# 24 of 36 expert blocks beside the top-key search in three rounded passes, split by ScalarE and GpSimd

## The chip, the cores and the metric

The kernel runs on one core of a Trainium2 chip. The metric is the device time of one launch in microseconds; the runs of one kernel are compared by their median.

## The reference, cut to what matters

Two blocks of a network follow each other over 256 tokens of width 1024. Each of the two layers of the second block ends in a product-key expert layer. Every token picks, for each of 8 heads, 16 of 16,384 experts, and only those count:

```python
cand_s = top_s[:, :, 0, :, None] + top_s[:, :, 1, None, :]      # 16 x 16 sums of the best keys of either half
best_s, best_pos = lax.top_k(cand_s.reshape(c, PEER_HEADS, -1), PEER_TOPK)
idx = jnp.take_along_axis(cand_i.reshape(c, PEER_HEADS, -1), best_pos, axis=-1)
gate = jax.nn.softmax(best_s, axis=-1)
ue = u[idx]
ve = v[idx]
act = jax.nn.gelu(jnp.einsum('td,thkd->thk', xc, ue).astype(jnp.float32), approximate=False)
return jnp.einsum('thk,thkd->td', (gate * act).astype(xc.dtype), ve)
```

## The kernel before, in words

The kernel gathers no rows. It computes the products of all tokens with all experts, densely, in 128 blocks of 128 experts, and multiplies by a matrix G that holds the gates and is zero elsewhere. A block has a u part (dot products of 256 tokens with 128 experts), a gelu, a product with its slice of G, and a v part (128 rows of 1024 added up, times the gated values).

In each layer l the expert layer goes through these stages, in this order on TensorE:

1. `wq`: the query projection, then the key scores (L2237), copied out of PSUM by ScalarE (L2345).
2. `pre`: the u parts of `EARLY` = 32 blocks, two to a chunk of weights, 16 chunks. These are plain float32 products of the weights as they landed with the float32 tokens `HX` (L2247). ScalarE applies the gelu (L2352). Meanwhile VectorE searches the best keys (function `top16`: L2421 to L2431), first over 128 keys in two turns, each framed by copies (L2442, L2445, L2446); then it adds the pairs of best keys in 16 additions (L2452), searches again over 256 sums, and works out indices and gates (L2460 to L2486). Its last step lets TensorE turn the indices around (L2254).
3. `mid`: G is built, 64 groups of four tokens, from one-hot matrices that VectorE (L2502), GpSimd (L2414) and ScalarE (L2373, L2375) write and TensorE multiplies (L2279). ScalarE copies out the part of G whose gelu does not exist yet (L2388); VectorE multiplies the part of the 32 early blocks with the gelus that `pre` left there (L2493). Between the groups TensorE does the u parts of `MID` = 8 more blocks (L2265).
4. `peer`: the `MAIN` = 88 other blocks, u part and v part in one go (L2316, L2318, L467 to L469).
5. `post`: the v parts of the 40 blocks whose u parts were done in `pre` and `mid`.

Products in `wq`, `peer` and `post` are made of three passes. ScalarE writes a rounded copy of a quarter of a chunk (a unit of 512 columns, L446), VectorE the remainder (L451), both into the buffer `SPLIT` with room for 4 units, and TensorE multiplies high by high, high by low and low by high. A chunk is 1 MB, four lie in the ring `wring`, and the SyncE queue loads the next one when `chunk_done` of its slot is raised: by TensorE in `pre` and `mid`, by VectorE behind the last remainder in the others. The semaphores `split_hi`, `split_lo` and `unit_used` count units written, remainders written and units used.

`HX_A` and `HX_B` are copies of the tokens for `mid`, written by ScalarE ahead of the early gelus (L2346, L2347). `HX_A` and the one-hot matrices lie in the same memory as `SPLIT`. GpSimd has nothing to do between the rotary tables, loaded once near a fifth of the span, and the first one-hot matrices of `mid`.

Of the kernel before, what the change touches and what calls it, by code (L numbers as in the profile page):

```python
# [16 lines left out]
ALU = mybir.AluOpType  # L17
# [8 lines left out]
T = 256  # L26
# [14 lines left out]
ROWS = 2 * PEER_HEADS  # L41
TOP = 16
BLOCKS = NKEYS
EARLY, MID = 32, 8
KEPT = MID + EARLY
MAIN = BLOCKS - KEPT
ALPHA = (2 * DEPTH) ** 0.25
# [36 lines left out]
def program(nc, A, out):  # L84
    ctx = ExitStack()
    with ctx:
# [287 lines left out]
        def turns(e, n):  # L374

            full, rest = divmod(n, RING)
            if full > 1:
                with e.Fori(0, full) as i:
                    for j in range(RING):
                        yield i, j  # L380
            else:
                for j in range(full * RING):
                    yield 0, j
            for j in range(rest):
                yield full, j
# [16 lines left out]
        def wait_done(e, name, i, j):  # L402
            s, r = slot_of(name, i, j)
            e.wait_ge(chunk_done[s], r + 2)
# [15 lines left out]
        def stream_pairs(sp, name, src, first, n):  # L420
            for i, j in turns(sp, n):
# [2 lines left out]
                sp.dma_start(wring[:, s, :].rearrange("p (a c) -> p a c", a=2),  # L424
                             src[first + RING * i + j]).then_inc(w_landed[s], 16)

        SPLIT_PHASES = [(name, n if name[:4] != "proj" else 17 - SPLIT_FROM) for name, n, _ in PHASES
                        if name != "ada" and name[:3] not in ("pre", "mid")]
        split_first, at = {}, 0
        for name, n in SPLIT_PHASES:  # L430
            split_first[name] = at
# [2 lines left out]
        def unit_of(name, i, q):  # L434

            return split_first[name] + UNITS * RING * i + q

        def raw_quarter(name, i, j, q):
            return wring[:, slot_of(name, i, j)[0], q * UNIT:(q + 1) * UNIT]
# [8 lines left out]
        def lo_quarter(v, name, i, j, q, n, buf, last):  # L448

            v.wait_ge(split_hi, n + 1)  # L450
            v.tensor_tensor(SPLIT[:, buf, 1, :], raw_quarter(name, i, j, q), SPLIT[:, buf, 0, :].bitcast(F32),  # L451
                            ALU.subtract).then_inc(split_lo, 1)
            if last:
                v.drain().then_inc(chunk_done[slot_of(name, i, j)[0]], 1)
# [67 lines left out]
        def hi_chunk(act, name):  # L522
            def work(i, j):
                for q in range(UNITS):
                    hi_quarter(act, name, i, j, q, unit_of(name, i, UNITS * j + q), q)
            return work
# [13 lines left out]
        def wait_product(e, name, i, j):  # L540

            e.wait_ge(unit_used, unit_of(name, i, UNITS * j + UNITS - 1) + 1 + UNITS)
# [1684 lines left out]
        def peer_tensor(pe, l):  # L2227
# [10 lines left out]
                                   WD["keys"], start=True, stop=True)  # L2238
                mm.then_inc(sc_done, 1)

            for i, j in turns(pe, EARLY // 2):
                w = wait_chunk(pe, f"pre{l}", i, j)
                b, u = bank_of(f"pre{l}", i, j)
                pe.wait_ge(bank_free[b], u + 1)
                for e in range(2):
                    for k in range(KT):
                        mm = pe.matmul(bank[b][:, e * T:(e + 1) * T], w[:, (e * KT + k) * P:(e * KT + k + 1) * P],  # L2247
                                       HX[:, k, :], start=(k == 0), stop=(k == KT - 1))
                mm.then_inc(chunk_done[slot_of(f"pre{l}", i, j)[0]], 1)
# [83 lines left out]
        def peer_scalar(act, l):  # L2333
            name = f"peer{l}"

            def drain_q(i, j):
                b, _ = bank_of(f"wq{l}", i, j)
                wait_product(act, f"wq{l}", i, j)
                act.activation(pairs(Q8)[:, j, :], bank[b][:, :], ACT.Copy).then_inc(bank_free[b], 1)

            ahead(act, 4, hi_chunk(act, f"wq{l}"), drain_q, started=True)
            act.drain().then_inc(q8_ready, 1)
            for f in range(8):
                act.wait_ge(sc_done, 8 * l + f + 1)
                act.activation(SC[:, 4 * f:4 * f + 4, :], view(bank[2 + f % 4][:, :], 4), ACT.Copy).then_inc(sc_in, 1)  # L2345
            act.activation(HX_A, HX[:, 0:5, :], ACT.Copy)  # L2346
            act.activation(HX_B, HX[:, 5:KT, :], ACT.Copy).then_inc(hx_kept, 1)  # L2347

            def early(i, j):
                b, _ = bank_of(f"pre{l}", i, j)  # L2350
                wait_done(act, f"pre{l}", i, j)
                act.activation(pairs(G)[:, (MAIN + MID) // 2 + RING * i + j, :], bank[b][:, :], ACT.Gelu).then_inc(bank_free[b], 1)  # L2352

            last = EARLY // 2 // RING - 1
            with act.Fori(0, last) as i:
                for j in range(RING):
                    early(i, j)
            early(last, 0)
            act.wait_ge(gate_in, l + 1)
            act.activation(IJG[:, 0, :], IJG[:, 0, :], ACT.Exp).then_inc(gate_exp, 1)  # L2360
            for j in range(1, RING):
                early(last, j)
            for tt in range(2):
                act.wait_ge(ijt_done, 2 * l + tt + 1)
                a = act.activation(PAIR[:, :, tt * P:(tt + 1) * P], view(bank[2 + tt][:, 0:3 * P], 3), ACT.Copy)  # L2365
            a.then_inc(pair_ready, 1)
            act.drain()

            def hots_scalar(n):

                act.wait_ge(g_done, GROUPS * l + n + 1)
                t = 4 * (n % 2) + 1
                act.activation(NEAR[:, n % 2, :], iota, ACT.Abs, scale=-1.0, bias=pair[:, 2, n // 2, t, :])  # L2373
                act.drain()
                act.activation(OHB[:, t, :], NEAR[:, n % 2, :], ACT.Relu, scale=-1.0, bias=ones[:, 0:1]).then_inc(hot_c, 1)  # L2375

            def mid_out(e):
                b, _ = bank_of(f"mid{l}", 0, e)
                wait_done(act, f"mid{l}", 0, e)
                act.activation(pairs(ACTX)[:, e, :], bank[b][:, :], ACT.Gelu).then_inc(bank_free[b], 1)  # L2380

            hots_scalar(0)
            hots_scalar(1)
            for n in range(GROUPS):
                if n + 2 < GROUPS:
                    hots_scalar(n + 2)
                act.wait_ge(g_done, GROUPS * l + n + 3)
                act.activation(G4[:, n, :, 0:MAIN + MID], view(bank[4 + n % 4][:, :], 4)[:, :, 0:MAIN + MID],  # L2388
                               ACT.Copy).then_inc(g_in, 1)
                if n % 16 == 1 and n > 1:  # L2390
                    mid_out(n // 16 - 1)
            mid_out(MID // 2 - 1)
            if l + 1 < DEPTH:
                act.drain()
                act.dma_start(wide_t[:], A["wide"][l + 1]).then_inc(wide_in, 16)

            def gelu(i, j):
                b, _ = bank_of(name, i, j)
                act.wait_ge(dots_ready, MAIN * l + RING * i + j + 1)
                act.activation(GA, GA, ACT.Gelu).then_inc(bank_free[b], 1)  # L2400

            peer_units(act, name, lambda *a: hi_quarter(act, name, *a),
                       begin=lambda: act.wait_ge(unit_used, unit_of(name, 0, 2) + UNITS), after=gelu)
            act.activation(TSD[:, 0:1], C["epsh"], ACT.Sqrt)
            for i, j in turns(act, KEPT // 2):
                hi_chunk(act, f"post{l}")(i, j)

        def peer_pool(pool, l):
            pool.wait_ge(pair_ready, l + 1)
# [24 lines left out]
        def peer_vector(v, l):  # L2434
# [89 lines left out]
            def gate(i, j):  # L2524
# [7 lines left out]
                v.drain()  # L2532
                v.tensor_tensor(g_lo, GA, g_hi.bitcast(F32), ALU.subtract).then_inc(gp_ready, 1)  # L2533

            peer_units(v, name, lambda i, j, q, n, buf: lo_quarter(v, name, i, j, q, n, buf, q == 3), middle=dots, late=gate)
            name = f"post{l}"

# [10 lines left out]
            def post(i, j, mid):  # L2548
                for q in range(UNITS):
                    if q % 2 == 0:  # L2550
                        kept(i, j, q // 2, mid)
                    lo_quarter(v, name, i, j, q, unit_of(name, i, UNITS * j + q), q, q == UNITS - 1)

            for j in range(MID // 2):
                post(0, j, True)
            with v.Fori(0, EARLY // 2 // RING) as i:
                for j in range(RING):
                    post(i + 1, j, False)

        block = ctx.enter_context(nc.Block())  # L2560

# [34 lines left out]
        @block.gpsimd  # L2596
        def _(pool):
            pool.wait_ge(ada_rows, ADA_EARLY)
            pool.dma_start(hyc_t[:, 0:hyc_n - T], A["hyc"][:, 0:hyc_n - T]).then_inc(hyc_in, 16)
            with pool.Fori(0, ADA_LATE) as c:  # L2600
                pool.wait_ge(late_done, c + 1)
                pool.dma_start(LATE, A["w_ada"][ADA_EARLY + c]).then_inc(late_landed, 16)
            squares_pool(pool)
            pool.wait_ge(part_lo, 3 * UNITS)
            pool.dma_start(rope_t, A["rope"]).then_inc(rope_in, 16)
            for l in range(DEPTH):
                peer_pool(pool, l)

        @block.scalar
# [260 lines left out]
```

## Time and profile before

| | |
|---|---|
| median of 3 runs | 3173.22 us (3163.9 to 3174.16) |
| the profiled run, its own time | 3169.45 us |
| its span in the trace | 3167.8 us |
| TensorE, VectorE, ScalarE, GpSimd busy | 3037.3, 2368.0, 1508.8, 216.3 us |

The profile is one execution. TensorE's busy time counts matmuls that overlap in the pipeline, so 96% busy is not 96% of its peak. All times of the trace are counted from the start of the span. A float32 matmul stands in the trace as two instructions. Layer 0's expert stages lie from 1196 to 2045 us, those of layer 1 some 1107 us later.

### The profile page before, as it was taken

What the parts mean: (1) busy time and instruction counts of PE and PEld (TensorE: products, weight loads), DVE (VectorE), ACT (ScalarE), POOL (GpSimd) and SP (SyncE); (2) the same over time, 40 slices, a digit from 0 to 9 for tenths busy, and PEclk for the clock granted to TensorE, in tenths of its full rate; (3) what the DMA queues carried; (4) which work ended last, traced back from release to release, by engine and by line L of the source; (5) the groups of instructions that cost most, each with busy time, mean ns of one, the idle gap of its engine ahead of it and who ended that gap; (6) DMA issues with size and microseconds to landing.
All of it is one profiled execution on the core that took longest, in us unless ns stands there. A gap on an engine that the chain in (4) does not pass through costs nothing.

```text
span 3167.8 us, 50781 instructions
## 1 busy us (share of the span) xinstructions
PE 3037.3 (96%) x16104; PEld 2527.0 (80%) x16104; DVE 2368.0 (75%) x5173; ACT 1508.8 (48%) x2634; POOL 216.3 (7%) x348
## 2 busy tenths in 40 slices
PE   7999999989989899999999999998999999999998
PEld 4888887869887779877888888777788778888887
DVE  5778787456657767997777777677679977777776
ACT  3222223245744652295555554446523955555544
POOL 0000000000000000190000000000001910000000
PEclk9999999999999999999999999999999999999999
DMA  7333333224222234314555555533343145555553
GB/s 271 105 114 105 114 117 109 80 73 145 80 94 105 99 130 135 131 41 159 187 188 190 189 186 188 170 107 107 120 141 125 41 146 185 186 189 189 190 188 131
DMA packets 73920, 439.61 MB, mean 139 GB/s; under 512 B 7184, under 2 KB 8720, under 8 KB 31824
## 3 DMA queue, kind: packets, MB, share of 16 engines
q1 hardware_dynamic: 71136, 419.15, 38.1%
q0 software_dynamic: 2528, 18.02, 1.6%
q8 instruction: 65, 1.06, 0.1%
q10 hardware_dynamic: 144, 0.98, 0.1%
q14 instruction: 47, 0.39, 0.0%
HBM read 437.08 MB, written 1.05 MB: 138 GB/s over the span
## 4 chain that ended last, share of the span: by engine, by line
PE 77%; DVE 15%; ACT 2%; DVEq 2%; issue 2%; ACTq 0%; DMA 0%; POOL 0%; SPq 0%
PE bank L467 16%; PE bank L469 16%; PE bank L468 16%; PE bank L2316 10%; PE bank L2318 5%; DVE arena L2502 2%; PE bank L2279 1%; DVE arena L1557 1%; PE bank L875 1%; DVE arena L2431 1%; DVE arena L2424 1%; DVE arena L2425 1%; PE bank L1505 1%; PE bank L864 1%; PE bank L1225 1%
## 5 line engine op out<-in xcount | busy, mean ns | idle before, releaser
L446 ACT ACTIVATE peer_r<-wring 128x512 fp32r<-128x512 f32 x1280 | 797.7, 631 | 797.5 <-PE bank L469 517.8
L451 DVE TENSOR_TENSOR peer_r<-wring,peer_r 128x512 fp32r<-128x512 f32 x1280 | 870.1, 692 | 408.9 <-ACT peer_r L446 405.6
L2316 PE MATMUL bank<-res_r,peer_r 128*128 128x512 f32 x1408 | 502.7, 397 | 3.4 <-DVE peer_r L451 3.4
L467 PE MATMUL bank<-h_r,peer_r 128*128 128x512 f32 (+1 forms) x1088 | 397.6, 365 | 22.6 <-DVE h_r L662 16.0
L467 PE MATMUL bank<-peer_r 128*128 128x512 f32 x1024 | 404.7, 395 | 3.2 <-DVE peer_r L2533 3.2
L469 PE MATMUL bank<-peer_r 128*128 128x512 f32 x1024 | 401.5, 392 | 0.0
L468 PE MATMUL bank<-peer_r 128*128 128x512 f32 x1024 | 399.6, 390 | 0.0
L2318 PE MATMUL bank<-res_r,peer_r 128*128 128x256 f32 x1408 | 394.9, 280 | 0.0
L469 PE MATMUL bank<-h_r,peer_r 128*128 128x512 f32 (+1 forms) x1088 | 385.4, 354 | 0.0
L468 PE MATMUL bank<-h_r,peer_r 128*128 128x512 f32 (+1 forms) x960 | 335.0, 349 | 0.0
L2316 PEld LDWEIGHTS bank<-res_r,peer_r 128*128 128x128 f32 x1408 | 264.5, 188 | 67.1 <-DVE peer_r L451 4.0
L2414 POOL TENSOR_SCALAR arena<-const_t,arena 128x128 f32<-128x128 f32 x320 | 198.6, 635 | 1679.4 <-ACT arena L2365 1666.6
L2318 PEld LDWEIGHTS bank<-res_r,peer_r 128*128 128x128 f32 x1408 | 265.6, 189 | 6.7
L467 PEld LDWEIGHTS bank<-h_r,peer_r 128*128 128x128 f32 x1088 | 207.5, 191 | 68.9 <-issue 36.9
L469 PEld LDWEIGHTS bank<-h_r,peer_r 128*128 128x128 f32 x1088 | 207.4, 191 | 28.2
L467 PEld LDWEIGHTS bank<-peer_r 128*128 128x128 f32 x1024 | 192.1, 188 | 47.0 <-DVE peer_r L2533 3.1
L469 PEld LDWEIGHTS bank<-peer_r 128*128 128x128 f32 x1024 | 192.1, 188 | 46.0
L2247 PE MATMUL bank<-arena,wring 128*128 128x256 f32 x1024 | 221.3, 379 | 0.0
L468 PEld LDWEIGHTS bank<-peer_r 128*128 128x128 f32 x1024 | 192.6, 188 | 36.0
L2247 PEld LDWEIGHTS bank<-arena,wring 128*128 128x128 f32 x1024 | 194.6, 190 | 26.5
L468 PEld LDWEIGHTS bank<-h_r,peer_r 128*128 128x128 f32 x960 | 183.3, 191 | 23.6 <-issue 2.4
L2279 PEld LDWEIGHTS bank<-arena 128*128 128x128 f32 x1024 | 127.7, 195 | 59.4 <-DVE arena L2502 52.8
(388 smaller groups left out, 4582.1 us busy)
## 6 DMA issues: line engine op xcount, KB each, us to landing
wring<-in_w_peer SPq DMA_DIRECT2D x256, 1024.0 KB, 4.9
wring<-in_w_proj SPq DMA_DIRECT2D x34, 1024.0 KB, 4.9
wring<-in_w_hy SPq DMA_DIRECT2D x32, 1024.0 KB, 5.1
arena<-in_w_ada POOLq DMA_DIRECT2D x16, 1024.0 KB, 5.2
wring<-in_w_out SPq DMA_DIRECT2D x16, 1024.0 KB, 4.9
wring<-in_w_ada SPq DMA_DIRECT2D x8, 1024.0 KB, 11.2
wring<-in_w_hyout SPq DMA_DIRECT2D x8, 1024.0 KB, 4.9
wring<-in_w_q SPq DMA_DIRECT2D x8, 1024.0 KB, 4.9
```

Of the source, the lines that this page charges most:

```text
L446: act.activation(SPLIT[:, buf, 0, :], raw_quarter(name, i, j, q), ACT.Copy).then_inc(split_hi, 1)
L451: v.tensor_tensor(SPLIT[:, buf, 1, :], raw_quarter(name, i, j, q), SPLIT[:, buf, 0, :].bitcast(F32), ALU.subtract).then_inc(split_lo, 1)
L467: pe.matmul(out_ap, w_hi, x_hi, start=start, stop=False, **kw)
L468: pe.matmul(out_ap, w_hi, x_lo, start=False, stop=False, **kw)
L469: return pe.matmul(out_ap, w_lo, x_hi, start=False, stop=stop, **kw)
L864: mm = pe.matmul(bank[b][:, f * 256:(f + 1) * 256], HC[m][:, f * P:(f + 1) * P], UT[:, part * 256:(part + 1) * 256], start=True, stop=True)
L2247: mm = pe.matmul(bank[b][:, e * T:(e + 1) * T], w[:, (e * KT + k) * P:(e * KT + k + 1) * P], HX[:, k, :], start=(k == 0), stop=(k == KT - 1))
L2279: mm = pe.matmul(bank[4 + b][:, s * P:(s + 1) * P], OHA[:, t, :], OHB[:, t, :], start=True, stop=True)
L2316: pe.matmul(two_parts(acc[:, :]), SPLIT[:, buf, 0, w], h_both[:, k, :, :], start=(k == 0), stop=False, skip_group_check=True)
L2318: mm = pe.matmul(acc[:, T:2 * T], SPLIT[:, buf, 1, w], h_hi[:, k, :], start=False, stop=(k == KT - 1), skip_group_check=True)
L2414: a = pool.tensor_scalar(OHB[:, 4 * half + s, :], iota, pair[:, 2, i, 4 * half + s, :], None, ALU.is_equal)
L2502: a = v.tensor_scalar(OHA[:, t, :], iota, pair[:, 1, 2 * i + b // 2, t, :], pair[:, 0, 2 * i + b // 2, t, :], ALU.is_equal, ALU.mult)
```

## The change

`EARLY` grows from 32 to 36, so `pre` has 18 chunks and `MAIN` shrinks from 88 to 84 blocks; `post` has 44. The first `PRE_SPLIT` = 12 chunks of `pre` (24 blocks) are done in three passes: ScalarE rounds the weights (`hi_chunk`), GpSimd writes the remainders in place of VectorE (`pre_pool`), TensorE runs `chunk3` with `h_hi` and `h_lo2`. GpSimd raises `chunk_done` for these chunks. The other 6 chunks stay as they were. ScalarE rounds the first chunk ahead of the score copies and writes `HX_A` only when the split chunks are through, because `SPLIT` is in use until then. The exponential of the gates moves to behind the gelu of chunk 14.

```diff
-EARLY, MID = 32, 8
+EARLY, MID = 36, 8
+PRE_SPLIT = 12
...
+        split_chunks = lambda name, n: {"proj": 17 - SPLIT_FROM, "pre": PRE_SPLIT}.get(name[:-1], n)
...
-            for i, j in turns(pe, EARLY // 2):
+            name = f"pre{l}"
+            for i, j in turns(pe, PRE_SPLIT):
+                chunk3(pe, name, i, j, h_hi, h_lo2, T, KT)
+            name = f"peer{l}"
+            for n in range(PRE_SPLIT, EARLY // 2):
+                i, j = divmod(n, RING)
                 w = wait_chunk(pe, f"pre{l}", i, j)
...
+            pre_hi = hi_chunk(act, f"pre{l}")
+            pre_hi(0, 0)
             for f in range(8):
                 act.wait_ge(sc_done, 8 * l + f + 1)
                 act.activation(SC[:, 4 * f:4 * f + 4, :], view(bank[2 + f % 4][:, :], 4), ACT.Copy).then_inc(sc_in, 1)
-            act.activation(HX_A, HX[:, 0:5, :], ACT.Copy)
-            act.activation(HX_B, HX[:, 5:KT, :], ACT.Copy).then_inc(hx_kept, 1)
+            act.activation(HX_B, HX[:, 5:KT, :], ACT.Copy)
...
+            ahead(act, PRE_SPLIT, pre_hi, early, started=True)
+            act.activation(HX_A, HX[:, 0:5, :], ACT.Copy).then_inc(hx_kept, 1)
+            for n in range(PRE_SPLIT, EARLY // 2):
+                early(*divmod(n, RING))
+                if n == EARLY // 2 - 4:
+                    act.wait_ge(gate_in, l + 1)
+                    act.activation(IJG[:, 0, :], IJG[:, 0, :], ACT.Exp).then_inc(gate_exp, 1)
...
+        def pre_pool(pool, l):
+            name = f"pre{l}"
+            pool.wait_ge(split_lo, unit_of(name, 0, 0))
+            for i, j in turns(pool, PRE_SPLIT):
+                for q in range(UNITS):
+                    n = unit_of(name, i, UNITS * j + q)
+                    pool.wait_ge(split_hi, n + 1)
+                    pool.tensor_tensor(SPLIT[:, q, 1, :], raw_quarter(name, i, j, q), SPLIT[:, q, 0, :].bitcast(F32),
+                                       ALU.subtract).then_inc(split_lo, 1)
+                pool.drain().then_inc(chunk_done[slot_of(name, i, j)[0]], 1)
...
+            v.wait_ge(split_lo, unit_of(name, 0, -2))
             peer_units(v, name, lambda i, j, q, n, buf: lo_quarter(v, name, i, j, q, n, buf, q == 3), middle=dots, late=gate)
```

VectorE's loop over the early blocks in `post` is written for 18 chunks instead of whole rings, and `pre_pool` is called ahead of `peer_pool` in each layer.

## Rows read from the trace of the kernel before

**Rows 1.** the page, parts 1 and 4: busy engines, chain that ended last.

```profile
PE 3037.3 (96%) x16104; PEld 2527.0 (80%) x16104; DVE 2368.0 (75%) x5173; ACT 1508.8 (48%) x2634; POOL 216.3 (7%) x348
...
PE 77%; DVE 15%; ACT 2%; DVEq 2%; issue 2%; ACTq 0%; DMA 0%; POOL 0%; SPq 0%
```

**Rows 2.** stretches of layer 0: early blocks, gate matrix, main blocks, last blocks.

```profile
core 0: us, PE busy (x) PEld busy (x) DVE busy (x) ACT busy (x) POOL busy (x), PEclk, DMA share, GB/s
1217.00:1329.30 112.30, 111.18 (x518) 97.39 (x516) 107.25 (x424) 19.57 (x27) 0.00 (x0) 1.00 0.43 142
1329.30:1434.00 104.70, 98.70 (x630) 76.67 (x630) 100.18 (x350) 94.80 (x195) 98.76 (x160) 0.98 0.11 40
1460.00:1900.00 440.00, 440.00 (x2203) 369.71 (x2202) 342.88 (x630) 232.14 (x394) 0.00 (x0) 1.00 0.54 188
1940.00:2044.00 104.00, 104.00 (x460) 86.15 (x459) 75.61 (x158) 47.46 (x75) 0.00 (x0) 1.00 0.59 193
```

**Rows 3.** TensorE in order of time, early blocks; start us, length us, what.

```profile
1209.63 7.17 PE L2237 MATMUL bank<-wide_t,arena 128*128 128x256 f32 x32 [0.72 <-ACTq L2342]
1216.64 110.67 PE L2247 MATMUL bank<-arena,wring 128*128 128x256 f32 x512
1327.85 0.87 PE L2254 MATMUL bank<-const_t,arena 128*128 128x128 f32 x6 [0.54 <-DVEq L2486]
```

**Rows 4.** VectorE in order of time, the same stretch of layer 0.

```profile
1217.69 1.23 DVE L2442 COPY arena<-arena 128x2048 f32 x1 [13.08 <-ACT arena L2345]
...
1239.57 1.23 DVE L2442 COPY arena<-arena 128x2048 f32 x1 [0.29 <-issue]
...
1261.06 5.45 DVE L2452 TENSOR_TENSOR arena<-arena 128x256 f32<-128x256 f32 x16
```

**Rows 5.** TensorE in three passes over 256 columns, query projection.

```profile
1199.75 0.28 PE L467 MATMUL bank<-res_r,peer_r 128*128 128x256 f32 x1
1199.87 0.28 PE L468 MATMUL bank<-res_r,peer_r 128*128 128x256 f32 x1
```

**Rows 6.** VectorE once a main block (L2531) and once a last block (L2544).

```profile
1922.14 0.29 DVE L2531 CAST peer_r<-arena 128x256 fp32r<-128x256 f32 x1
...
1927.74 0.29 DVE L2531 CAST peer_r<-arena 128x256 fp32r<-128x256 f32 x1
...
1937.75 0.29 DVE L2544 CAST peer_r<-arena 128x256 fp32r<-128x256 f32 x1
...
1940.47 0.29 DVE L2544 CAST peer_r<-arena 128x256 fp32r<-128x256 f32 x1
```

**Rows 7.** all engines but TensorE around one GpSimd addition of 512 columns.

```profile
580.90 1.29 POOL L628 TENSOR_TENSOR arena<-arena 128x512 f32<-128x512 f32 x1 [78.59 <-ACT arena L623]
...
581.37 1.37 DVE L451 TENSOR_TENSOR peer_r<-wring,peer_r 128x512 fp32r<-128x512 f32 x1 [1.22 <-ACT peer_r L446]
...
583.89 0.69 DVE L451 TENSOR_TENSOR peer_r<-wring,peer_r 128x512 fp32r<-128x512 f32 x1 [1.15 <-ACT peer_r L446]
```

**Rows 8.** groups by line: x count, busy us, mean ns of one.

```profile
L451 DVE TENSOR_TENSOR peer_r<-wring,peer_r 128x512 fp32r<-128x512 f32 x1280 | 870.1, 692 | 408.9 <-ACT peer_r L446 405.6 <-issue 0.8
L446 ACT ACTIVATE peer_r<-wring 128x512 fp32r<-128x512 f32 x1280 | 797.7, 631 | 797.5 <-PE bank L469 517.8 <-PE bank L2318 275.9 <-issue 3.6
...
L2414 POOL TENSOR_SCALAR arena<-const_t,arena 128x128 f32<-128x128 f32 x320 | 198.6, 635 | 1679.4 <-ACT arena L2365 1666.6 <-PE bank L2279 7.7
...
L2502 DVE TENSOR_SCALAR arena<-const_t,arena 128x128 f32<-128x128 f32 x512 | 153.4, 361 | 10.8 <-PE bank L2279 3.8 <-ACT arena L2365 3.3 <-issue 2.2
...
L2493 DVE TENSOR_TENSOR arena<-bank,arena 128x128 f32 (+1 forms) x128 | 52.9, 413 | 5.3 <-ACT arena L2388 4.4
...
L2452 DVE TENSOR_TENSOR arena<-arena 128x256 f32<-128x256 f32 x32 | 10.9, 418 | 0.3
```

**Rows 9.** stretches around a TensorE idle, columns as in rows 2.

```profile
646.60:655.60 9.00, 0.00 (x0) 0.00 (x0) 7.75 (x7) 4.39 (x8) 0.00 (x0) 0.62 0.00 0
655.60:659.00 3.40, 3.04 (x7) 1.96 (x7) 3.20 (x5) 3.09 (x6) 0.00 (x0) 0.50 0.00 0
```

More of the change, by code:

```diff
@@ L425, in stream_pairs @@
                              src[first + RING * i + j]).then_inc(w_landed[s], 16)
-        SPLIT_PHASES = [(name, n if name[:4] != "proj" else 17 - SPLIT_FROM) for name, n, _ in PHASES
-                        if name != "ada" and name[:3] not in ("pre", "mid")]
+        split_chunks = lambda name, n: {"proj": 17 - SPLIT_FROM, "pre": PRE_SPLIT}.get(name[:-1], n)
+        SPLIT_PHASES = [(name, split_chunks(name, n)) for name, n, _ in PHASES if name != "ada" and name[:3] != "mid"]
         split_first, at = {}, 0
@@ L2345, in peer_scalar @@
                 act.activation(SC[:, 4 * f:4 * f + 4, :], view(bank[2 + f % 4][:, :], 4), ACT.Copy).then_inc(sc_in, 1)
-            act.activation(HX_A, HX[:, 0:5, :], ACT.Copy)
-            act.activation(HX_B, HX[:, 5:KT, :], ACT.Copy).then_inc(hx_kept, 1)
+            act.activation(HX_B, HX[:, 5:KT, :], ACT.Copy)
             def early(i, j):
                 b, _ = bank_of(f"pre{l}", i, j)
-                wait_done(act, f"pre{l}", i, j)
+                if isinstance(i, int) and RING * i + j >= PRE_SPLIT:
+                    wait_done(act, f"pre{l}", i, j)
+                else:
+                    wait_product(act, f"pre{l}", i, j)
                 act.activation(pairs(G)[:, (MAIN + MID) // 2 + RING * i + j, :], bank[b][:, :], ACT.Gelu).then_inc(bank_free[b], 1)
[L2354 to L2362, printed above, removed]
+            ahead(act, PRE_SPLIT, pre_hi, early, started=True)
[5 more added lines that the diff above has]
+                    act.activation(IJG[:, 0, :], IJG[:, 0, :], ACT.Exp).then_inc(gate_exp, 1)
             for tt in range(2):
@@ L2555, in peer_vector @@
                 post(0, j, True)
-            with v.Fori(0, EARLY // 2 // RING) as i:
-                for j in range(RING):
-                    post(i + 1, j, False)
+            for i, j in turns(v, EARLY // 2):
+                post(i + 1, j, False)
         block = ctx.enter_context(nc.Block())
@@ L2606, in _ @@
             for l in range(DEPTH):
+                pre_pool(pool, l)
                 peer_pool(pool, l)
```

## The prediction

> **What bounds the kernel now.** I began with the page's busy times and its chain [rows 1]: TensorE carries 77% of the chain that ended last, VectorE 15%, GpSimd nothing; GpSimd is busy 7% of the span. Any block that leaves TensorE's critical stages is time saved. Then I cut layer 0 into its stages [rows 2]. In the main and the last blocks TensorE is busy in every microsecond (440 of 440, 104 of 104). Building G, VectorE is busy 100.2 of 104.7 us, and the 64 groups take 104.7 / 64 = 1.64 us each. The stage that the change edits, from 1217 to 1329 us, is different: TensorE 111.2 and VectorE 107.3 of 112.3 us, side by side. TensorE in order of time shows which is later [rows 3]: the early blocks end at 1216.64 + 110.67 = 1327.3 us, and TensorE then waits 0.54 us for VectorE's last step. So this stage has two limits within about half a microsecond of each other, and VectorE's is the later one. Whatever delays VectorE here delays the layer in full.
>
> **What is saved behind the search.** Once a main block, VectorE comes round every 1927.74 - 1922.14 = 5.60 us; once a last block, every 1940.47 - 1937.75 = 2.72 us [rows 6]. A block that moves from `peer` to `pre` keeps its v part and loses 5.60 - 2.72 = 2.88 us of a TensorE-bound stage. Four blocks in two layers: 8 x 2.88 = 23.0 us saved.
>
> **What it costs in the stage that builds G.** VectorE's L2493 now covers 36 blocks for 4 tokens, 144 columns instead of 128. A `tensor_tensor` takes 692 ns at 512 columns and 418 at 256 [rows 8], 1.07 ns a column, so 16 columns are 17 ns, on the engine that sets the pace there. 64 groups x 2 layers x 0.017 = 2.2 us. ScalarE's copy gets 16 columns shorter, worth nothing.
>
> **TensorE in the edited stage.** Before: 16 chunks in 110.67 us, 6.92 us each [rows 3]. In three passes over 256 columns, matmuls follow each other every 0.12 us [rows 5], and a chunk has 16 x 3 = 48 of them: 5.76 us, if its units are ready. 12 x 5.76 + 6 x 6.92 = 69.1 + 41.5 = 110.6 us. TensorE does 18 chunks in the time of 16; this term is 0, and the split part would end at about 1216.6 + 69.1 = 1285.7 us.
>
> **Is the splitting fast enough?** A unit must be ready every 1.44 us. ScalarE rounds one in 0.63 us [rows 8] beside a gelu of some 0.6 us a chunk: well inside. GpSimd's `tensor_tensor` over 512 columns took 1.29 us [rows 7]; four are 5.2 us, leaving 0.6 us a chunk for waits and the drain. It keeps up, barely. The store in the rounded type is not in the trace; the nearest row is VectorE's, with no surcharge visible, so I take 1.29. The bounds: no surcharge, or 25%, about what would make GpSimd slower than TensorE. At the start four roundings of 0.63 us now stand in front of the eight score copies. TensorE makes one score bank in 7.17 / 8 = 0.90 us [rows 3] and a copy needs about 0.6, so a start 2.5 us late less 1.3 us already waiting is caught up over eight copies: 0, at most 2.5 us a layer. Queued behind are VectorE's first copy at 1217.69 [rows 4] and everything after it. `HX_A` moves behind the 12th gelu, where ScalarE is idle most of each chunk. GpSimd's queue held nothing else; SyncE gets its slots back sooner.
>
> **What GpSimd does to VectorE.** This is the term that decides. Rows 7 hold the collision: GpSimd adds from 580.90 to 582.19; a VectorE subtraction starts at 581.37 and takes 1.37 us instead of the 0.69 of the next one. It ends 0.55 us after GpSimd does, about the 512 x 1.07 ns of its data. So it stood still until GpSimd was through. GpSimd lost nothing. Against that, 320 one-input GpSimd operations (0.64 us) ran beside 512 one-input VectorE operations of 0.36 us in the stage that builds G [rows 8]: no such doubling. A VectorE operation that reads two tensors waits for a GpSimd operation under way; one that reads one tensor does not. The searches (MAX8, FIND_INDEX8, MATCH_REPLACE8) read one and should stay as they are. Two kinds in the window of GpSimd's work, 1210 to some 1284 us, do not look safe.
>
> The 16 additions L2452 read two tensors. Alone they take 5.45 us, 0.34 each [rows 4]. Once one is held, a GpSimd operation is waiting when it ends, takes its turn, and holds the next. GpSimd runs at most three units ahead of TensorE, so at 1265 us (TensorE in unit 33 or 34 of 48) some 11 of its units are still to start; each holds one addition for 1.0 to 1.29 us (1.29 less what GpSimd sets up during the addition). I take 1.2: 11 x 1.2 = 13.2, and 0.9 for the first. 14.1 us.
>
> The copies L2442 (two) and L2445, L2446 (two each) read one tensor, but fast: 1.23 us for 2048 columns is 0.6 ns a column [rows 4] against 1.07 for the additions, so they draw two words a step as an addition does. No row shows one beside GpSimd. Bounds: 0 or 1.29 us each. By the nearest likeness, the addition, I count five of the six (GpSimd is idle at 1217.69) at 0.8 us: 4.0 us.
>
> The Trainium skill, SBUF — State Buffer, section "Who interferes with whom", says of this pair that the second one to start "fully blocks", for VectorE operations with two SBUF inputs and for copies in its fast mode. By that rule the copies too would wait, and the sum is the one taken; without the rule's copies it would be 8 us lower. Rows 7 agree for two inputs.
>
> Sum: 18.1 us a layer, 36.2 us in both, all on the path, since VectorE is already last. The gates reach ScalarE 18 us later (at about 1316 us), with TensorE still in chunk 16, so that wait hides.
>
> **TensorE's clock.** TensorE would stand idle from 1327 to about 1346 us. After 9 us of idleness the granted clock was at 0.62 and then 0.50 (1.2 of 2.4 GHz) for 3.4 us of work [rows 9]. The same behind the new gap costs half of 3.4 us: 1.7 a layer, 3.4 us; 0 if VectorE's pace hides it.
>
> **The sum.** -23.0 + 2.2 + 36.2 + 3.4 = +18.8 us. Against the profiled run's own 3169.45 us: 3188.3. The median of the runs shown is 3.8 us above that run; I forecast on the median: 3173.2 + 18.8 = 3192 us, 0.6% slower.
>
> **Rivals.** (a) The additions run in a row: VectorE, which has its next addition at hand 0.08 us before the last one's record ends, keeps its turn, and GpSimd waits once. Then a layer costs 4.0 + 0.9 + at most 0.3, say 5.2 us; GpSimd is 5.4 us late, 2 us of which its lead covers, so TensorE ends 3 us later, hidden by VectorE. -23.0 + 2.2 + 10.4 = -10.4: 3163 us. That is the other side; it decides when fewer than about four additions of 16 are held. For it speaks the tight spacing, against it that GpSimd is always waiting by then.
> (b) VectorE isn't held at all, the queueing in rows 7 being peculiar to those operations: -20.8, 3152 us. Rows 7 speak against it (one of five alike).
> (c) GpSimd needs over 1.44 us a unit, say 1.6 with rounding store and drain. TensorE's part grows by 12 x 4 x 0.16 = 7.7 us, but more units are left when the additions come, so all 16 are held for 1.5 us: 4.5 + 24 = 28.5 us a layer. -23.0 + 2.2 + 57 + 3.4 = +39.6: 3213 us.
>
> **Chances and range.** A difference under 0.3% (9.5 us) can't be told from none here. Forecast 0.60, own range 3180 to 3202 (an addition held for 1.0 to 1.29 us, copies held or not). (a) 0.22, (b) 0.08, (c) 0.10. 0.3% faster is 3163.7: (a) lies on that line and gives 0.13 faster, 0.09 same; (b) is faster. Of the forecast 0.04 ends within 0.3%, the rest above. Faster 0.21, same 0.13, slower 0.66. The range 3158 to 3204 takes in (a) and the forecast's upper bound.
>
> **What would show it.** In the profile after: the L2452 group, 10.9 us over 32 [rows 8], at some 40 us; L2445 and L2446 above 0.29 us; the searches unchanged; TensorE's split chunks 5.8 us apart; GpSimd 1.29 us a unit; a TensorE wait of some 18 us for VectorE before L2254, with a clock near one half behind it; 84 main blocks of 5.60 us. Additions at 0.42 us each would prove the sum wrong by its largest term; split chunks above 6 us would mean (c).

## The result, and the profile after

The changed kernel takes 3183.82 us (median of 7 runs, 3182.62 to 3189.37) where the kernel before, on the same chips, takes 3168.15 (7 runs, 3163.9 to 3174.16): a ratio of 1.0048, 95% interval 1.0037 to 1.0059, or 15.7 us slower (the interval is 12 to 19 us).

The page of the changed kernel: span, busy times, GpSimd by fortieths of the span, and engines on the chain that ended last.

```profile
span 3186.7 us, 51783 instructions
...
PE 3021.9 (95%) x16488; PEld 2532.2 (79%) x16488; DVE 2388.3 (75%) x5141; ACT 1553.8 (49%) x2712; POOL 338.7 (11%) x444
...
POOL 0000000000000006192000000000061920000000
...
PE 75%; DVE 16%; DVEq 3%; ACT 3%; issue 2%; ACTq 0%; DMA 0%; POOL 0%; SPq 0%
```

TensorE's share of the chain fell by 2 points and VectorE's rose by 1 [rows 1]; GpSimd holds 0% of the chain although it causes the delay, because the chain names the engine that was working (or standing) last, and that was VectorE.

TensorE in order of time around the early blocks of layer 0; the last bracket is its idle time and who ended it.

```profile
1212.80 6.96 PE L2238 MATMUL bank<-wide_t,arena 128*128 128x256 f32 x31 [0.72 <-ACTq L2348]
...
1288.92 41.60 PE L2253 MATMUL bank<-arena,wring 128*128 128x256 f32 x192
1348.45 1.54 PE L2260 MATMUL bank<-const_t,arena 128*128 128x128 f32 x6 [17.93 <-DVEq L2505]
```

Before, the same two points lay 118.2 us apart and TensorE waited 0.54 us for VectorE [rows 3]. Now they are 135.7 us apart and it waits 17.93 us. TensorE's own part did not grow: the 12 split chunks run from 1219.62 to 1288.92 us without an idle stretch, 5.78 us each, and the six plain ones take 41.60 us, 110.9 us together.

VectorE in the same stretch: copies at 1220.86 to 1243.91 and 1265.80, 1266.84, then the 16 additions.

```profile
1220.86 1.23 DVE L2461 COPY arena<-arena 128x2048 f32 x1 [13.08 <-ACT arena L2353]
...
1241.70 0.97 DVE L2464 COPY arena<-arena 128x256 f32 x1 [0.19 <-issue]
1242.59 1.39 DVE L2465 COPY arena<-arena 128x256 uint32 x1
1243.91 2.31 DVE L2461 COPY arena<-arena 128x2048 f32 x1
...
1265.80 1.11 DVE L2464 COPY arena<-arena 128x256 f32 x1 [0.17 <-issue]
1266.84 1.41 DVE L2465 COPY arena<-arena 128x256 uint32 x1
1268.39 18.73 DVE L2471 TENSOR_TENSOR arena<-arena 128x256 f32<-128x256 f32 x16
```

The two copies ahead of the additions, in the kernel before:

```profile
1260.37 0.29 DVE L2445 COPY arena<-arena 128x256 f32 x1 [0.18 <-issue]
1260.62 0.29 DVE L2446 COPY arena<-arena 128x256 uint32 x1
```

The additions take 18.73 us where they took 5.45, the copies of 256 columns 1.0 to 1.4 us where they took 0.3, the second large copy 2.31 for 1.23 [rows 4]. The first large copy, with GpSimd idle, is unchanged. In layer 1 the additions take 19.66 us. There the second large copy started at the same time as a unit of GpSimd and was not held: it took 1.22 us, and GpSimd's unit took 2.38 for its usual 1.30. So either side can be the one that waits.

GpSimd while the additions run; each row is one chunk of four units.

```profile
1262.94 5.16 POOL L2423 TENSOR_TENSOR peer_r<-wring,peer_r 128x512 fp32r<-128x512 f32 x4 [0.57 <-ACT peer_r L447]
1268.36 5.62 POOL L2423 TENSOR_TENSOR peer_r<-wring,peer_r 128x512 fp32r<-128x512 f32 x4 [0.26 <-ACT peer_r L447]
1274.23 5.84 POOL L2423 TENSOR_TENSOR peer_r<-wring,peer_r 128x512 fp32r<-128x512 f32 x4 [0.26 <-ACT peer_r L447]
1280.34 5.84 POOL L2423 TENSOR_TENSOR peer_r<-wring,peer_r 128x512 fp32r<-128x512 f32 x4 [0.26 <-issue]
```

Twelve units fall into the 18.7 us of the additions, about 1.5 us apart, where an undisturbed chunk takes 5.1 to 5.2 us. GpSimd loses 0.5 to 0.7 us a chunk; VectorE loses 13.3 us in all. One by one, 12 of the 16 additions take about 1.5 us. The other four take 0.41 us, as alone: they start while GpSimd is between two chunks, or behind its last unit.

Groups of VectorE and GpSimd over both layers: count, then busy us and mean ns of one.

```profile
L2471 DVE TENSOR_TENSOR arena<-arena 128x256 f32<-128x256 f32 x32 | 38.4, 1272 | 0.3
...
L2443 DVE FIND_INDEX8 arena<-arena 128x8 uint32<-128x128 f32 (+1 forms) x96 | 31.6, 329 | 0.0
L2444 DVE MATCH_REPLACE8 arena<-arena 128x128 f32<-128x128 f32 (+1 forms) x96 | 30.7, 319 | 0.0
...
L2461 DVE COPY arena<-arena 128x2048 f32 x4 | 6.0, 1495 | 26.2 <-ACT arena L2353 26.2
...
L2465 DVE COPY arena<-arena 128x256 uint32 x4 | 5.6, 1397 | 0.0
...
L2464 DVE COPY arena<-arena 128x256 f32 x4 | 4.0, 988 | 0.7 <-issue 0.7
...
L2423 POOL TENSOR_TENSOR peer_r<-wring,peer_r 128x512 fp32r<-128x512 f32 x96 | 127.1, 1354 | 1442.9 <-ACT peer_r L447 1440.7 <-issue 1.8
```

And the two searching operations of the kernel before, for comparison.

```profile
L2424 DVE FIND_INDEX8 arena<-arena 128x8 uint32<-128x128 f32 (+1 forms) x96 | 31.7, 331 | 0.0
L2425 DVE MATCH_REPLACE8 arena<-arena 128x128 f32<-128x128 f32 (+1 forms) x96 | 30.8, 321 | 0.0
```

The searches cost what they cost before (329 against 331 ns, 319 against 321). Two thirds of them, those over 128 keys, ran while GpSimd was splitting. So of what ran beside GpSimd here, the additions of two tensors and the fast copies are held, and the searches are not.

The first microseconds behind TensorE's wait, by stretches.

```profile
core 0: us, PE busy (x) PEld busy (x) DVE busy (x) ACT busy (x) POOL busy (x), PEclk, DMA share, GB/s
1330.50:1348.40 17.90, 0.03 (x1) 0.00 (x0) 17.37 (x9) 0.60 (x1) 0.00 (x0) 0.58 0.19 59
1348.40:1357.00 8.60, 5.82 (x24) 5.27 (x25) 4.19 (x14) 3.96 (x9) 4.91 (x8) 0.50 0.00 0
1357.00:1361.00 4.00, 3.86 (x26) 3.16 (x26) 3.35 (x12) 3.42 (x9) 3.34 (x6) 0.95 0.02 4
```

The granted clock is at 0.58 in the gap and 0.50, 1.2 of 2.4 GHz, for 8.6 us behind it, then near full. The kernel before has a slow stretch here too, though a shorter one: 0.50 in the 3.4 us from 1331.4 in layer 0, and 0.51 in the 6.9 us from 2437.3 in layer 1, where the changed kernel has 0.50 in the 9.3 us from 2464.2.

By stages, from the first score product (L2237 before, L2238 after) to the turning of the indices (L2254, L2260), from there to the first product behind G (L2291, L2297), and from there to layer 1's first score product or, in layer 1, to the end, in us for layers 0 and 1:

| kernel | scores and early blocks | G | main and last blocks |
|---|---|---|---|
| before | 118.2, 117.8 | 108.8, 111.6 | 880.3, 621.5 |
| after | 135.7, 135.2 | 111.7, 112.5 | 868.8, 610.0 |
| difference | +17.4, +17.4 | +3.0, +0.9 | -11.5, -11.5 |

34.8 + 3.9 - 23.0 = 15.7 us. That this is also the difference of the two medians is in part luck, since single runs of one kernel differ by up to 10 us. The spans of the two profiled runs differ by 3.2 us more. That much lies ahead of the first stage that the change touches (1212.80 against 1209.63 us) and is scatter: in the ten profiles of this case the first score product starts anywhere from 1205.6 to 1214.3 us, and in the three without the split at 1209.6, 1213.1 and 1214.3.

### The profile page after: what moved, and what is told of

Same layout as the page of the kernel before. It is cut to its first block, busy times and chain, and to the rows that moved or that the text cites. A ratio compares the mean times of both kernels' runs of the same rounds, so it can differ in the third digit from the quotient of the medians.

```text
span 3186.7 us, 51783 instructions
## 1 busy us (share of the span) xinstructions
PE 3021.9 (95%) x16488; PEld 2532.2 (79%) x16488; DVE 2388.3 (75%) x5141; ACT 1553.8 (49%) x2712; POOL 338.7 (11%) x444
## 4 chain that ended last, share of the span: by engine, by line
PE 75%; DVE 16%; DVEq 3%; ACT 3%; issue 2%; ACTq 0%; DMA 0%; POOL 0%; SPq 0%
PE bank L468 16%; PE bank L470 16%; PE bank L469 16%; PE bank L2322 10%; PE bank L2324 5%; DVE arena L2521 2%; DVE arena L2471 1%; DVE arena L1558 1%; PE bank L1506 1%; DVE arena L2450 1%; DVE arena L2443 1%; DVE arena L2444 1%; PE bank L876 1%; PE bank L865 1%; PE bank L1226 1%
## 5 line engine op out<-in xcount | busy, mean ns | idle before, releaser
L447 ACT ACTIVATE peer_r<-wring 128x512 fp32r<-128x512 f32 x1360 | 846.8, 631 | 839.4 <-PE bank L470 569.8
L452 DVE TENSOR_TENSOR peer_r<-wring,peer_r 128x512 fp32r<-128x512 f32 x1264 | 857.5, 691 | 402.1 <-ACT peer_r L447 398.5
L2322 PE MATMUL bank<-res_r,peer_r 128*128 128x512 f32 x1344 | 479.9, 397 | 3.4 <-DVE peer_r L452 3.4
L2324 PE MATMUL bank<-res_r,peer_r 128*128 128x256 f32 x1344 | 376.9, 280 | 0.0
L2322 PEld LDWEIGHTS bank<-res_r,peer_r 128*128 128x128 f32 x1344 | 252.5, 188 | 64.3 <-DVE peer_r L452 4.0
L2423 POOL TENSOR_TENSOR peer_r<-wring,peer_r 128x512 fp32r<-128x512 f32 x96 | 127.1, 1354 | 1442.9 <-ACT peer_r L447 1440.7
L2324 PEld LDWEIGHTS bank<-res_r,peer_r 128*128 128x128 f32 x1344 | 253.5, 189 | 6.4
L2285 PE MATMUL bank<-arena 128*128 128x128 f32 x1024 | 150.7, 291 | 17.7 <-DVE arena L2521 10.0
```

The costliest lines, as they stand in the source:

```text
L447: act.activation(SPLIT[:, buf, 0, :], raw_quarter(name, i, j, q), ACT.Copy).then_inc(split_hi, 1)
L2285: mm = pe.matmul(bank[4 + b][:, s * P:(s + 1) * P], OHA[:, t, :], OHB[:, t, :], start=True, stop=True)
L2322: pe.matmul(two_parts(acc[:, :]), SPLIT[:, buf, 0, w], h_both[:, k, :, :], start=(k == 0), stop=False, skip_group_check=True)
L2324: mm = pe.matmul(acc[:, T:2 * T], SPLIT[:, buf, 1, w], h_hi[:, k, :], start=False, stop=(k == KT - 1), skip_group_check=True)
L2423: pool.tensor_tensor(SPLIT[:, q, 1, :], raw_quarter(name, i, j, q), SPLIT[:, q, 0, :].bitcast(F32), ALU.subtract).then_inc(split_lo, 1)
```

## The experiments

All ratios are to the kernel before, run on the same chip. The first two take one suspect away each or keep it alone.

**GpSimd's operations made short.** Only 8 of 512 columns are subtracted; the remainders of the other columns of the 24 blocks are left out.

```diff
-pool.tensor_tensor(SPLIT[:, q, 1, :], raw_quarter(name, i, j, q), SPLIT[:, q, 0, :].bitcast(F32),
-                   ALU.subtract).then_inc(split_lo, 1)
+pool.tensor_tensor(SPLIT[:, q, 1, 0:8], raw_quarter(name, i, j, q)[:, 0:8],
+                   SPLIT[:, q, 0, 0:8].bitcast(F32), ALU.subtract).then_inc(split_lo, 1)
```

> GpSimd subtracts only the first 8 of the 512 columns of each unit in the stage of the early blocks; the remainders of the other 504 columns of these 24 blocks are left out. Counts, waits, roundings and TensorE's three passes stay. Theory (GpSimd's 1.3 us operations hold VectorE's two-input additions and its copies): the 16 additions go back to about 5.5 us from 18.7, the copies to 0.3 and 1.2 us, VectorE ends the stage about 17 us a layer sooner than in the changed kernel, and the whole is -23.0 + 2.2 = -20.8 us against the kernel before, ratio 0.993; up to 2 us more if the short operations still hold a few additions. Rival (three passes, ScalarE's new order or the later exponential cost the time): the time stays near the changed kernel's, ratio 1.005.

Measured: 3144.89 us, ratio 0.993 (0.9915 to 0.9945). The stage is back at 118.2 and 117.8 us. All engines but TensorE during the additions, the first three operations of GpSimd that meet them:

```profile
1260.51 5.48 DVE L2471 TENSOR_TENSOR arena<-arena 128x256 f32<-128x256 f32 x16
1261.63 0.37 POOL L2423 TENSOR_TENSOR peer_r<-wring,peer_r 128x8 fp32r<-128x8 f32 x1 [1.21 <-ACT peer_r L447]
1263.07 0.28 POOL L2423 TENSOR_TENSOR peer_r<-wring,peer_r 128x8 fp32r<-128x8 f32 x1 [1.07 <-ACT peer_r L447]
1264.57 0.46 POOL L2423 TENSOR_TENSOR peer_r<-wring,peer_r 128x8 fp32r<-128x8 f32 x1 [1.22 <-ACT peer_r L447]
```

The additions take 5.48 us. Here it is GpSimd that is held: its 0.20 us operations take 0.28 to 0.46 when they start inside an addition. Everything else of the change is in this kernel, so the 35 us that the two stages had grown by hang on the length of GpSimd's operations. Three passes, ScalarE's new order and the later exponential cost nothing that the length of the stage shows.

**The split without the moved blocks.**

```diff
-EARLY, MID = 36, 8
+EARLY, MID = 32, 8
```

> The split part of 12 chunks as in the changed kernel, but EARLY back at 32, so no block leaves the main stage. Theory: nothing is saved and VectorE is held as before, some 17.4 us a layer, and the gap in TensorE's work is longer, since it now ends its 16 chunks 13.8 us sooner, so about 2 us a layer go to its clock: 2 x 19.4 = +39 us, ratio 1.012. Rival (the size of the early part, not the split, costs the time): near the time before, ratio 1.000 to 1.003.

Measured: 3206.06 us, ratio 1.0109 (1.0094 to 1.0124). The stage takes 135.6 and 135.2 us, as in the changed kernel. TensorE in order of time at its end:

```profile
1319.28 9.87 PE L2253 MATMUL bank<-arena,wring 128*128 128x256 f32 x32 [10.95 <-ACT arena L2362]
1346.97 1.54 PE L2260 MATMUL bank<-const_t,arena 128*128 128x128 f32 x6 [17.82 <-DVEq L2505]
```

It waits 10.95 us for ScalarE, which stands at the late gates, and 17.82 us for VectorE, and none of this makes the stage longer: VectorE sets it. Behind the longer wait the granted clock is 0.50 from 1347.0 to 1355.5 us. Building G takes 110.2 and 110.6 us all the same, no more than in the undisturbed kernels with the same blocks (108.8 and 111.6; 110.4 and 110.6 in the one with one addition below). So TensorE's slow clock there cost nothing that this shows. The expected ratio of 1.012 lies inside the interval, with nothing of it left for the clock to explain: two longer stages of 17.4 us are 35 us, or 1.011.

**The moved blocks without the split.** 18 plain float32 chunks, the exponential behind the gelu of chunk 14.

```diff
-EARLY, MID = 32, 8
+EARLY, MID = 36, 8
```

> EARLY at 36 with no split at all: 18 plain float32 chunks, VectorE undisturbed. Theory: TensorE's part takes 18 x 6.92 = 124.5 us in place of 110.7 and becomes the later of the two, 13.3 us after VectorE's old end. -23.0 + 2.2 + 2 x 13.3 = +5.8 us, ratio 1.002. Rival (moved blocks save less than 2.88 us each, say half): +17 us, ratio 1.0055.

Measured: 3179.99 us, ratio 1.0033 (1.0024 to 1.0043).

```profile
1220.11 124.48 PE L2247 MATMUL bank<-arena,wring 128*128 128x256 f32 x576
1344.43 0.82 PE L2254 MATMUL bank<-const_t,arena 128*128 128x128 f32 x6
```

18 chunks take 124.48 us, 6.92 each, and TensorE no longer waits for VectorE: the stage is 131.3 us in both layers, 13.3 more than before on average, as expected. The expected ratio of 1.002 lies just outside the interval, so the expectation was missed by some 5 us. The stage of G explains about 1 of them (111.9 and 111.8 us) and the main and last blocks about 2 (869.6 and 611.3 us, 10.7 and 10.2 saved where 11.5 were counted). The rest stays open; it is of the size of the scatter. So without the split the moved blocks don't pay, and the half gain that the rival had them at (1.0055) lies outside the interval.

**One addition for 16.** Same numbers, one instruction.

```diff
-for a in range(TOP):
-    v.tensor_tensor(view(WK[:, a, 0, :], TOPK), wide(tv4[:, i, a, 0, :], 2, TOPK),
-                    wide(tv4[:, i, a, 1, :], 1, TOPK), ALU.add)
+v.tensor_tensor(WK[:, :, 0, :].rearrange("p a (k m) -> p a k m", m=TOPK), wide(tv4[:, i, :, 0, :], 3, TOPK),
+                wide(tv4[:, i, :, 1, :], 2, TOPK), ALU.add)
```

> The changed kernel with VectorE's 16 additions of 256 columns written as one of 4096 columns. Theory (each operation is held once by the GpSimd operation under way, whole operations taking turns): one hold of at most 1.3 us and 4.4 us of work in place of 18.7 us; GpSimd is kept out for 4.4 us, of which its lead covers 2. The copies stay held, 4.2 us. VectorE ends about 4 us a layer later than before the change: -23.0 + 2.2 + 8 = -13 us, ratio 0.996. Rival (the two engines share the path word by word, so the additions take 3.4 times their time however they are cut): the one addition takes about 15 us, +8 us, ratio 1.003.

Measured: 3155.12 us, ratio 0.9962 (0.9949 to 0.9975). GpSimd and VectorE at that place:

```profile
1260.65 1.44 POOL L2423 TENSOR_TENSOR peer_r<-wring,peer_r 128x512 fp32r<-128x512 f32 x1
1261.08 5.29 DVE L2470 TENSOR_TENSOR arena<-arena 128x4096 f32<-128x4096 f32 x1
1262.35 8.91 POOL L2423 TENSOR_TENSOR peer_r<-wring,peer_r 128x512 fp32r<-128x512 f32 x4 [0.26 <-ACT peer_r L447]
```

The addition starts at 1261.08 and GpSimd's unit ends at 1262.09; the addition ends at 1266.37, 4.3 us later. It was held once, for 1.0 us. A path shared word by word would have made it some 15 us, 3.4 times its own time like the 16. GpSimd stood still in its turn: its four units take 8.91 us for 5.1, and the price of that shows in TensorE's waits (who waited for whom, us, times, longest):

```profile
PE bank L468 <- POOL peer_r L2423: 1.9, 1, 1.9
...
PE bank L2260 <- DVEq L2504: 1.2, 1, 1.2
```

1.9 us of waiting for a remainder, 1.2 us for VectorE: the stage is 121.0 and 120.9 us, 3.0 above the old one where about 4 were expected.

**One addition in the kernel before.** The control: GpSimd is idle.

> The kernel before, with its 16 additions written as one: nothing of the change. GpSimd is idle there, so nothing is held. Theory: the one addition takes 4.4 us for 5.45, VectorE ends the stage 1.0 us sooner, and TensorE, which was 0.54 us ahead, becomes the last: 2 x 0.5 = 1 us less, ratio 0.9997. Rival (the one addition is worth several us by itself, and that explains its gain in the changed kernel): ratio below 0.998.

Measured: 3168.71 us, ratio 0.9994 (0.9983 to 1.0006). The stage takes 117.5 us in both layers, half a microsecond less, as expected. The one instruction is worth nothing that can be told from no change where nobody holds it; in the changed kernel it is worth some 27 us (1.0048 less 0.9962 of 3168).

**GpSimd writes and reads nothing.** The remainders of the 24 blocks are left out (zero), the loop of `pre_pool` is written out.

```diff
-pool.tensor_tensor(SPLIT[:, q, 1, :], raw_quarter(name, i, j, q), SPLIT[:, q, 0, :].bitcast(F32),
-                   ALU.subtract).then_inc(split_lo, 1)
+pool.memset(SPLIT[:, q, 1, :].bitcast(F32), 0.0).then_inc(split_lo, 1)
```

> GpSimd fills the 512 columns of each remainder with zero in place of the subtraction, its loop written out; the remainders of the 24 blocks are left out. GpSimd then writes the same cells and reads nothing. Theory, with the Trainium skill's SBUF page (Who interferes with whom): VectorE's two-input additions meet only a GpSimd operation that reads, so they take 5.5 us as alone, while the copies, which use both of VectorE's paths for reading and writing, may still be held for what is left of a fill. VectorE ends within 2 us of its old end: ratio 0.993 to 0.994. Rival (any GpSimd operation holds any two-input VectorE operation): 12 fills, each shorter than a subtraction, hold the additions again, by their length each: with 0.5 us, 6 us a layer, ratio about 0.997.

Measured: 3145.33 us, ratio 0.9922 (0.9899 to 0.9944). VectorE and GpSimd at the last copies and the additions:

```profile
1262.12 0.29 DVE L2463 COPY arena<-arena 128x256 f32 x1 [0.18 <-issue]
1262.37 0.71 DVE L2464 COPY arena<-arena 128x256 uint32 x1
1262.41 0.53 POOL L2423 MEMSET peer_r<- 128x512 f32 x1 [0.91 <-ACT peer_r L447]
...
1263.22 4.45 DVE L2470 TENSOR_TENSOR arena<-arena 128x256 f32<-128x256 f32 x13
1263.85 0.53 POOL L2423 MEMSET peer_r<- 128x512 f32 x1 [0.91 <-ACT peer_r L447]
...
1265.29 0.53 POOL L2423 MEMSET peer_r<- 128x512 f32 x1 [0.91 <-ACT peer_r L447]
```

The additions (13 in this window, in 4.45 us, 0.34 apart) run through the fills at 1263.85 and 1265.29 as if they were not there; all 32 of both layers take 0.41 or 0.42 us. The copy at 1262.37 meets the fill that ends at 1262.94 and takes 0.71 us for 0.29. In layer 1 a large copy meets another:

```profile
2335.37 0.53 POOL L2423 MEMSET peer_r<- 128x512 f32 x1 [0.92 <-ACT peer_r L447]
2335.45 1.53 DVE L2460 COPY arena<-arena 128x2048 f32 x1 [0.21 <-issue]
```

It takes 1.53 us for 1.23. Where a copy was under way first, the fill is the one that grows (0.63 to 0.75 us for 0.53, three times). These are few cases, but they agree: a copy is held by a GpSimd operation that only writes, an addition only by one that reads. The ratio agrees (the rival's 0.997 lies outside the interval, the expected 0.993 to 0.994 inside), and the rows show it directly.

**Fewer split chunks.**

```diff
-PRE_SPLIT = 12
+PRE_SPLIT = 8
```

> PRE_SPLIT at 8 in place of 12, EARLY still 36. GpSimd is through with its 32 units at about 1261 us, before the 16 additions start. Theory: the additions take 5.5 us, only the copies of the first half of the search are held (2 us), VectorE ends near 1330 us; TensorE's part is 8 x 5.76 + 10 x 6.92 = 115.3 us, 4.1 us after the stage's old end. -23.0 + 4 (stage of G as measured in the changed kernel) + 2 x 4.1 = -11 us, ratio 0.9966. Rival (the split costs in proportion to its units, two thirds of what 12 chunks cost): 2 x 17.4 x 2/3 = 23 us, ratio 1.001.

Measured: 3153.87 us, ratio 0.995 (0.9933 to 0.9967). GpSimd's last chunk, and VectorE behind it:

```profile
1249.70 5.50 POOL L2423 TENSOR_TENSOR peer_r<-wring,peer_r 128x512 fp32r<-128x512 f32 x4 [0.26 <-ACT peer_r L447]
```

```profile
1258.64 0.29 DVE L2464 COPY arena<-arena 128x256 f32 x1 [0.17 <-issue]
1258.89 0.29 DVE L2465 COPY arena<-arena 128x256 uint32 x1
1259.33 3.78 DVE L2471 TENSOR_TENSOR arena<-arena 128x256 f32<-128x256 f32 x11
```

GpSimd is through at 1255.2 us. The last copies take 0.29 us, and the additions follow at full pace; the copies of the first half are still held (1.01, 1.39 and 2.32 us). The stage is 122.1 us in both layers, 4.1 above the old one as expected: TensorE's own work, with no wait for VectorE. A third fewer units takes off not a third but nearly all of the holding, because only operations that run at the same time collide.

**The search in place, two additions.** The search reads the scores where they lie and writes its values and indices where they belong, so the copies L2461, L2464, L2465 and their like fall away.

```diff
-with v.Fori(0, 2 * ROWS // TOP) as i:
-    v.tensor_copy(WK[:, :, 0, 0:NKEYS], by_turn(SC)[:, i])
-    v.drain()
-    top16(v, NKEYS)
-    v.tensor_copy(by_turn(TV)[:, i], V16)
-    v.tensor_copy(by_turn(TIU)[:, i], I16)
+for i in range(2 * ROWS // TOP):
+    top16(v, NKEYS, by_turn(SC)[:, i], by_turn(TV)[:, i], by_turn(TIU)[:, i])
...
+for g in range(2):
+    u = slice(g * TOP // 2, (g + 1) * TOP // 2)
+    v.tensor_tensor(WK[:, u, 0, :].rearrange("p a (k m) -> p a k m", m=TOPK), wide(tv4[:, i, u, 0, :], 3, TOPK),
+                    wide(tv4[:, i, u, 1, :], 2, TOPK), ALU.add)
```

> The changed kernel with the search reading the scores where they lie and writing its results where they belong, so the copies fall away, and the 16 additions written as two of 2048 columns. Theory: VectorE needs about 8 us less than with one addition and copies, so TensorE decides with its 110.6 us and at most 1 us of waiting for a remainder while GpSimd stands behind an addition of 2.2 us. -23.0 + 4 + 1 = -18 us, ratio 0.9943. Rival (the search in place is slower, or the gap moves to another wait): no better than the one addition, 0.996.

Measured: 3151.14 us, ratio 0.994 (0.9922 to 0.9959), the fastest kernel here that computes everything, though its interval overlaps those of the one addition and of 8 split chunks. GpSimd's units and the two additions a layer:

```profile
L2424 POOL TENSOR_TENSOR peer_r<-wring,peer_r 128x512 fp32r<-128x512 f32 x96 | 129.3, 1381 | 1437.5 <-ACT peer_r L448 1434.3 <-issue 3.2
...
L2469 DVE TENSOR_TENSOR arena<-arena 128x2048 f32<-128x2048 f32 x4 | 12.5, 3174 | 0.3
```

An addition of 2048 columns takes 3.17 us in the mean, 2.2 of work and about 1 of holding; GpSimd's mean unit rises to 1.38 us. The stage takes 120.1 and 119.5 us: TensorE waits 1.8 and 1.6 us for remainders and no longer for VectorE. How much of the gain comes from the missing copies and how much from the two additions is not separated here.

## Why the prediction was right

**Saved blocks, -23.0 us.** Right: 880.3 to 868.8 us in layer 0, 621.5 to 610.0 in layer 1, -11.5 each. That it fits to the tenth is luck. Over all ten profiles, three with 32 early blocks and seven with 36, the means differ by 12.7 us in layer 0, where the single profiles scatter by up to 9 us, and by 11.4 in layer 1, where they scatter by 3.

**TensorE's 18 chunks in the time of 16, 0.** Right. The changed kernel needs 110.9 us for them without a wait, for 110.6 forecast and 110.7 before. With GpSimd's operations short the stage takes 118.2 and 117.8 us, as before. GpSimd kept up: four units in 5.1 us, no surcharge for the rounded store. That rules out rival (c), which needed over 1.44 us a unit. One sentence of this term was wrong without effect: a surcharge of 25% is not what would just make GpSimd slower than TensorE. 1.44 / 1.29 is 12%, so the margin was half of what the text says.

**Late start, 0.** Right: 8.06 us lie between the first score product and VectorE's first copy, before and after (1209.63 and 1217.69; 1212.80 and 1220.86).

**The holding, +36.2 us.** Measured 34.8 (17.4 a layer). Its parts in layer 0: the additions 18.73 - 5.45 = 13.3 where 14.1 were taken; the copies, from the shift of what follows them, 4.2 us where 4.0 were taken. In layer 1 they are 14.2 and, as what is left of the 17.4, 3.2 us, so that the two layers come out alike is chance. The copies were the unseen part of the sum, priced by likeness to the additions, and that likeness held, but for the one large copy in layer 1 that came first. The rule of the Trainium skill, SBUF — State Buffer, section "Who interferes with whom" ("fully blocks", for two inputs and for fast copies) agrees with the measured rows on both counts. So does what the same section of the Trainium skill says of a GpSimd operation that only writes: it leaves a two-input operation alone (0.34 us an addition beside fills).

**Whole operations in turn, not data in proportion.** This carried the forecast against rival (a). GpSimd's units follow each other through all of the additions, twelve of them, so VectorE did not keep its turn; and one addition in place of 16 was held once. Rival (b) is out by the same rows. Nor is it a matter of these buffers: in the kernel before, a GpSimd addition that neither reads nor writes `wring` or `SPLIT` holds a VectorE subtraction on them in the same way [rows 7].

**The stage of G, +2.2 and the clock, +3.4 us.** 3.9 us together for 5.6, both small against the scatter of this stage (108.8 to 111.6 us in the two layers of one profile). The three profiles with 32 early blocks have a mean of 110.4 us, the six with 36 and no long wait 111.1, the changed kernel 112.1. So the 16 columns cost some 0.7 us a layer where 1.1 were taken, and at most 1.0 is left for the clock. The clock did fall, and stayed low for 8.6 us rather than the 3.4 taken from [rows 9]; the prediction overlooked that the kernel before is slow there for 3.4 us too. The split without the moved blocks had the same low clock and no longer stage. So this term was sized too high, at 1.7 us a layer for something between 0 and 1.

**The sum.** 18.8 us forecast, 15.7 measured, in the medians and in the two profiles outside the stretch ahead of the change. Of the 3.1 us between them, 1.4 are the holding and 1.7 the stage of G with its clock. The absolute 3192 us rests on a median of three runs that was 5 us above the later one of seven; the change is the part to judge.

## What to carry to other kernels

Where a second engine is set beside VectorE, count how many VectorE operations of the kind that it holds start while it runs, and price each at a whole operation of the other engine: many short two-input operations or fast copies are the worst case. One long one is held once, here for 1.0 us, but keeps the other engine out for its whole length, here until TensorE waited 1.9 us. Moving work to an idle GpSimd can look right and still lose, and GpSimd's share of the chain was 0% here although it caused the delay; look instead for VectorE operations whose mean grew. Three cures were tried: one long operation in place of 16, GpSimd done ahead of the additions, and no copies together with two additions. They turned 0.5% lost into 0.4, 0.5 and 0.6% won.

## What the runs showed of the hardware that was not expected

A held operation costs both sides, whichever came second: 8-column GpSimd subtractions of 0.20 us took up to 0.46 inside additions, and GpSimd stood through nearly all of a 4.3 us addition (8.91 us for four units of 5.1). With both engines' queues full they take turns, one whole operation each. A copy is held even by a GpSimd fill that reads nothing (0.71 us for 0.29, 1.53 for 1.23), an addition is not. And a granted clock of 0.50 for 8.6 us of TensorE's work behind an idle of 17.9 us cost at most 1 us a layer in a stage in which VectorE sets the pace.
